# Moving the rounded weight buffers of a three-slot ring to other byte offsets in SBUF

## What is computed

```python
for l in range(2):
    x = x + 0.5 * (silu(h @ w_gate) * (h @ w_up)) @ w_down      # h = rms_norm(x), 2816 hidden
    x = x + concat(four attention mixers of rms_norm(x) @ w_in[l]) @ w_out[l]
    x = x + 0.5 * (silu(h @ w_gate2) * (h @ w_up2)) @ w_down2
    x = rms_norm(x)
# second block: h @ w_in_2 (7424 columns), a pooling mixer, two attention mixers,
# three gated projections, one output projection, a last rms_norm
```

## Time and profile before

| | us |
|---|---|
| median of 2 runs | 1316.11 |
| lowest, highest | 1311.11, 1321.1 |
| the profiled execution's own time | 1319.89 |
| its span, first to last instruction | 1317.6 |
| mean granted TensorE clock in it | 0.968 of full |

### The profile page before, as it was taken

The page is one execution under the profiler, slowest core; times in us unless marked ns, Lnnn a source line. Parts: engine busy times, 40 slices in busy tenths (PEclk is TensorE's granted clock), DMA queues, the critical chain, the costliest instruction groups (busy, mean ns, idle before and its releaser), DMA issues.

```text
span 1317.6 us, 24755 instructions
## 1 busy us (share of the span) xinstructions
PE 1265.6 (96%) x10500; PEld 1239.5 (94%) x10500; DVE 841.5 (64%) x1059; ACT 640.0 (49%) x850; POOL 78.7 (6%) x57
## 2 busy tenths in 40 slices
PE   6999999988999999999999997999999999999997
PEld 6999999978999999999999996899999989899995
DVE  5766677775676666876667686476666754446665
ACT  4433346754543334533335764453333554766542
POOL 1110011210000000000000211000000000000000
PEclk9999999986999999999999995799999999999999
DMA  8876665320565655566665530256655655415542
GB/s 287 219 227 206 191 224 172 114 87 2 182 200 193 191 191 192 170 199 195 194 219 163 166 132 12 65 165 219 192 191 191 200 178 174 128 58 168 176 152 105
DMA packets 169514, 220.33 MB, mean 167 GB/s; under 512 B 5280, under 2 KB 152480, under 8 KB 169312
## 3 DMA queue, kind: packets, MB, share of 16 engines
q1 hardware_dynamic: 165680, 213.66, 50.8%
q0 software_dynamic: 2080, 2.48, 1.0%
q10 hardware_dynamic: 1680, 3.13, 0.7%
HBM read 218.15 MB, written 3.42 MB: 168 GB/s over the span
## 4 chain that ended last, share of the span: by engine, by line
PE 86%; ACT 6%; DVE 5%; issue 1%; DMA 1%; SPq 0%; POOLq 0%; POOL 0%; DVEq 0%; ACTq 0%
PE pj L433 12%; PE pj L437 12%; PE pj L436 12%; PE acc L437 8%; PE acc L436 8%; PE acc L433 8%; PE tr L433 6%; PE tr L437 6%; PE tr L436 6%; PE acc L616 4%; ACT probs L994 2%; ACT w_hi L875 1%; PE tr L608 1%; DVE w_lo L1186 1%; PE tr L586 1%
## 5 line engine op out<-in xcount | busy, mean ns | idle before, releaser
L1186 DVE TENSOR_TENSOR w_lo<-raw,w_hi 128x2048 fp32r<-128x2048 f32 (+2 forms) x206 | 459.4, 2230 | 241.7 <-ACT w_hi L875 240.3
L875 ACT ACTIVATE w_hi<-raw 128x2048 fp32r<-128x2048 f32 (+2 forms) x206 | 381.2, 1854 | 395.3 <-PE pj L433 142.0
L433 PE MATMUL pj<-hT_hi,w_hi 128*128 128x256 f32 x992 | 277.2, 279 | 3.0 <-DVE w_lo L1186 2.4
L437 PE MATMUL pj<-hT_hi,w_lo 128*128 128x256 f32 x992 | 275.8, 278 | 0.0
L436 PE MATMUL pj<-hT_lo,w_hi 128*128 128x256 f32 x992 | 275.7, 278 | 0.0
L437 PE MATMUL acc<-act_hi,w_lo 128*128 128x256 f32 x704 | 194.3, 276 | 0.0
L433 PE MATMUL acc<-act_hi,w_hi 128*128 128x256 f32 x704 | 194.3, 276 | 0.0
L436 PE MATMUL acc<-act_lo,w_hi 128*128 128x256 f32 x704 | 194.3, 276 | 0.0
L433 PEld LDWEIGHTS pj<-hT_hi,w_hi 128*128 128x128 f32 x992 | 187.5, 189 | 4.5 <-DVE w_lo L1186 2.6
L436 PEld LDWEIGHTS pj<-hT_lo,w_hi 128*128 128x128 f32 x992 | 187.3, 189 | 0.0
L437 PEld LDWEIGHTS pj<-hT_hi,w_lo 128*128 128x128 f32 x992 | 187.1, 189 | 0.0
(11 more groups left out here) (212 smaller groups left out, 1989.6 us busy)
## 6 DMA issues: line engine op xcount, KB each, us to landing
raw<-in_w_in SPq DMA_DIRECT2D x47, 1024.0 KB, 5.3
raw<-in_ffn_w_up SPq DMA_DIRECT2D x44, 1024.0 KB, 5.3
raw<-in_ffn_w_down SPq DMA_DIRECT2D x44, 1024.0 KB, 5.0
raw<-in_ffn_w_gate SPq DMA_DIRECT2D x43, 1024.0 KB, 5.4
raw<-in_w_out SPq DMA_DIRECT2D x12, 1024.0 KB, 4.9
raw<-in_w_proj_a SPq DMA_DIRECT2D x4, 512.0 KB, 3.5
raw<-in_w_proj_b SPq DMA_DIRECT2D x4, 512.0 KB, 3.9
raw<-in_w_proj_c SPq DMA_DIRECT2D x4, 512.0 KB, 3.4
```

The costliest lines, as they stand in the source:

```text
L433: ins = pe.matmul(out, lhs[0], rhs[0], start=first, stop=False, **kw)
L437: return pe.matmul(out, lhs[1], rhs[0], start=False, stop=last, **kw)
L875: act.activation(w_hi[r % RING][:, 0:w], raw[r % RING][:, 0:w], ACT.Copy).then_inc(hi_set, 1)
L1186: dve.tensor_tensor(w_lo[r % RING][:, 0:w], raw[r % RING][:, 0:w], w_hi[r % RING][:, 0:w].bitcast(F32), ALU.subtract).then_inc(lo_set, 1)
```

## The change

Three unused tensors of 16, 64 and 32 float32 values are allocated, each ahead of one slot's buffers, and the order of the buffers changes from three `w_hi` and then three `w_lo` to `w_hi0 w_lo0`, `w_hi1 w_lo1`, `w_hi2 w_lo2`. By the same sum as above the buffers of slot 0 then start at 384 modulo 512 (161664 and 169856), those of slot 1 at 128 (178304 and 186496), those of slot 2 at 256 (194816 and 203008). `raw` stays at 320. The last byte used moves from 210752 to 211200. No instruction, wait or semaphore is added or removed.

```diff
         raw = [sb(f"raw{i}", [P, SLOT]) for i in range(RING)]
-        w_hi = [sb(f"w_hi{i}", [P, SLOT], F32R) for i in range(RING)]
-        w_lo = [sb(f"w_lo{i}", [P, SLOT], F32R) for i in range(RING)]
+
+        w_hi, w_lo = [], []
+        for i, gap in enumerate((16, 64, 32)):
+            sb(f"gap{i}", [P, gap])
+            w_hi.append(sb(f"w_hi{i}", [P, SLOT], F32R))
+            w_lo.append(sb(f"w_lo{i}", [P, SLOT], F32R))
```

## The result

| | before | after |
|---|---|---|
| median, us | 1316.11 | 1360.64 |
| lowest, highest (2 runs each) | 1311.11, 1321.1 | 1360.64, 1360.65 |
| span of the profiled execution | 1317.6 | 1358.4 |
| ratio after/before, 95% interval | | 1.033 [1.027, 1.039] |

The changed kernel is slower by 3.3%. The prediction, no change, was wrong, and 1360.6 lies above its range of 1290 to 1347. The spans differ by 40.8 us, the medians by 44.5; the rest is that the profiled execution of before lay 3.8 us above its median.

The account below looks back on a forecast made before the run. TensorE's matmul pace was taken to bound the kernel; gaps, weight offset, raw offset and halves side by side each counted 0 us, leaving the median of 1316 us. Range 1290 to 1347, the likeliest case's own 1310 to 1322.

Parts of the forecast that it names:

- What bounds the kernel: Whole kernel: TensorE, busy 96% of the span, sets the time by its matmul pace; preparation and DMA keep ahead.
- the stated signal of a wrong forecast: Feed-forward slots: the forecast is wrong if paces differ between gate, up and down slots.
- rival 1: 256-column matmuls: offsets free reads down to the weight load's floor, 25 us less, 1291; whole or in part, chance 0.24.
- I take zero: Offset of weights against activations in 256-column matmuls: priced at 0 us, as opposite distances show the same two paces.
- The two sweeps that seemed to show a flat cost: 160-column projection, mean 111.7 ns across four offsets, and float32 matmuls, 1.68 against 1.67 us: offset costs nothing there.
- Nothing in the trace is slower than the slow pace: Upper bound on a bad offset: the slow pace everywhere at full clock, 4.5 ns more per fast matmul.
- if one of the three slots costs 9 ns or more: Another way to lose beyond 2%: one slot's 2,970 matmuls at 9 ns or more each, 27 us.
- Rival 3: Feed-forward stages: nearer reads bring the slow pace, 31 us more, 1347; in full or worse, chance 0.16.
- Rival 2: 256-column matmuls: the extra is wholly collision, all come to 108.8 ns, 51 us less, 1265; chance 0.05.
- Rival 4: Buffer placement: tensors could be placed by another rule, so nothing changes; included in no change, chance 0.50.
- the weight load's floor of 111.7: 256-column matmuls: lowest pace in ns set by a 128-column weight load, taken from the 160-column projection.
- The rule of the Trainium skill: TensorE operand reads: two independent ports, PE never waits, so no offset matters and the change is worth 0 us.

Follow-up runs that it names:

- Experiments 7: Against the kernel before: old buffer order, one gap putting all weight buffers at offset 448 modulo 512; 1341.7 us, ratio 1.018.
- 9: Against the kernel before: old buffer order, one gap putting all weight buffers at offset 192; 1343.9 us against 1319.9.
- 6: Against the kernel before: old buffer order, one gap putting all weight buffers at offset 64; 1321.7 us against 1317.4, ratio 1.001.
- 10: Against the kernel before: slots with stationary weights stay at offset 320, slots with moving weights start at 448; 1316.4 us against 1319.9, ratio 0.999.
- experiment 1: Against the kernel before: halves of each slot side by side, no gaps, all weights still at 320; 1318.4 us against 1318.1, ratio 1.002.
- experiment 2: Against the kernel before: old buffer order, one gap putting all six weight buffers at offset 256; 1368.4 us, span 1366.1.

## Why the prediction was wrong, point by point

**What bounds the kernel: right.** TensorE's pace is the time, nothing else came near, and the stated signal of a wrong forecast came: paces that differ by buffer. The number of matmuls was right too, in part by luck: in before some 6,840 stand at 113.3 ns and some 2,270 at 117.8, where the prediction had 6,838 and 2,250. Sharing out the rest evenly, as its text says, would have given about 910 fast and 2,090 slow outside the feed-forward stages, and not 750 and 2,250. It makes 1 us in rival 1.

**"I take zero: both roles sit at opposite distances now (320 and 192) and show the same two paces": this step failed.** The term that it put at 0 us measured 44.5 us between the medians. Both roles do show both paces, but not in the same shares. Where weights are stationary in the feed-forward stages, all slots from the fourth on stood at 113.3; of the 6,088 matmuls of those windows 216 belong to the token projection that follows, whose first slot runs on at 113.4. In the token projections, where they move, the trace of before has 117.8 in nearly all slots but the first of a stage; some of them lie in the earlier trace rows, from 228.4 us. I had put the difference down to how a stretch begins. It was the effect of the sign, 320 against 192, that I wrote "should have told them apart", and it did. Experiments 7 and 9 show it: with the offset at 448 or 192 the two roles change places. The start of a stretch matters as well (6 and 10), but a whole feed-forward stage at 113.3 was only seen at 64 and 320. And even two roles with equal shares would not have proved the term zero: 320 and 192 are both odd multiples of 64, and the change went to even ones, where the runs show 118.6 to 119.9 ns in place of 113.3, 36 us in the feed-forward stages alone.

**The two sweeps that seemed to show a flat cost did not test the change.** The 160-column projection stands at 320, 448, 64 and 192, all odd multiples of 64, where the change goes to even ones; and at 111.7 ns it has the slack that the text names. It stayed at 110.8 to 111.0 ns over its 48 matmuls in every kernel here, also in the changed one, where its chunks start at 384, 0, 128 and 256. The float32 matmuls take 1.67 / 7 = 0.24 us each, twice as long. The text named the slack and the half pace and still counted both rows as evidence. They were none: a cost of full-pace reads has to be read from full-pace reads.

**"Nothing in the trace is slower than the slow pace": too low a bound.** As the trace of before holds one offset only, its slowest row bounds nothing about another. 4.5 ns per matmul became 5.3 (384), 5.5 (128) and 6.6 (256), and the stretches that were slow already lost 0.8 to 2.1 ns. The nearest I came was "if one of the three slots costs 9 ns or more", a price for a single slot. The top of the range, 1347, came from this bound: 6,838 × 4.5 = 31 us. With the measured mean of 5.7 the feed-forward stages alone give 36 us.

**Rival 3 had the right sign and the wrong reason.** It said that a read nearer to the other, 128 bytes instead of 192, could fall into the slower pace. Nearness is not it: 64 is as good as 320, and 256, the farthest, is the worst of the round offsets at 120.0. Nor was it the slower of the two paces of before that took over: 384, 128 and 256 have paces of their own, the same in each stage.

**Rivals 1, 2 and 4 are out.** At none of twelve distances did a stream of 256-column products come under 113.3 at full clock, so neither the weight load's floor of 111.7 nor 108.8 can be had by offset. And the paces followed the offsets that the sum of sizes gives, so the tensors lie there.

**The rule of the Trainium skill.** Every kernel here issues the same matmuls on the same data, and at full clock the pace goes from 113.3 to 123.3 ns with the addresses alone. "SBUF — State Buffer", section "Who interferes with whom", has two independent read ports and a PE that never waits on anyone. By that rule the spans of experiments 1 and 2, 1315.9 and 1366.1, would have been equal but for the 10 us or so that the clock moves; the measurement decides against it, at least as a rule that addresses don't matter.

**Right and worth nothing to the sum:** ScalarE and VectorE kept their times with inputs and outputs at any of the offsets, and the halves side by side cost nothing (experiment 1).

**What stays open.** The runs say which distances are good, not what in the hardware makes them so; no row shows it. Whether the 16 and 32 bytes of 304, 336, 288 and 352 count as distance or as the weights' own alignment was not separated. What decides which of the two paces a stage takes at a good distance was not found, nor could it be made to happen.

## What to carry to other kernels

When matmuls follow each other without waits, measure the distance from start to start and treat the start addresses of both operands as part of the kernel: here only stationary minus moving equal to 64 modulo 256 bytes held 113.3 ns over whole feed-forward stages, and a new tensor ahead of a buffer can take that away for 3% of the time. One bad distance in three matmuls, or one bad slot in three, is enough to lose it for the others too. Before a mixed pace is put down to chance, compare its shares role by role; a difference in shares can be the effect itself, as it was here.

## What the runs showed of the hardware that I had not expected

- The pace depends on where the operands start down to 16 bytes: 113.3 ns at 320, 118.7 at 336, 117.7 to 123.3 at 304.
- A stage can hold either of two paces for 160 us with the same addresses and the same kind of slots (113.3 and 117.8 at offset 64).
- With 512 moving columns the order is another one. The last output projection takes (1336.40 - 1335.01) / 6 = 232 ns after, by its timeline, and with all offsets at 256 (experiment 2) (1345.80 - 1345.12) / 3 = 227 ns; at 320 and at 448 for all it is 233.3. There are only 96 such matmuls. After, then experiment 2:

```profile
1335.01 0.39 PE L437 MATMUL acc<-w_hi,hT_hi 128*128 128x512 f32 x1
...
1336.40 0.39 PE L437 MATMUL acc<-w_hi,hT_hi 128*128 128x512 f32 x1
```

```profile
1345.12 0.39 PE L434 MATMUL acc<-w_hi,hT_hi 128*128 128x512 f32 x1
...
1345.80 0.39 PE L434 MATMUL acc<-w_hi,hT_hi 128*128 128x512 f32 x1
```

- The stretches of short matmuls in the mixing stages took 212.3 and 199.5 us in two executions with equal pace elsewhere, at a mean granted clock of 0.84 and 0.81 against 0.86 and 0.88.
